# Products nobody reads, put into TensorE's long waits of a two-layer hybrid backbone

## The chip, the cores and the metric

The kernel is one program on one core of one Trainium2 chip. It is written against the engines directly: TensorE (PE in the profile, its weight loads PEld), VectorE (DVE), ScalarE (ACT), GpSimd (POOL) and SyncE (SP, which issues most DMAs) each have their own instruction list and meet only at semaphores. The metric is the device time of one execution in microseconds (us), from the first to the last instruction. Before the change it is 1954.93 us, the median of three runs (1952.61 to 1957.86).

## The reference

Two layers over 256 latent and 256 context tokens, width 1024. Each layer normalizes, projects to four mixers (attention, a long convolution by a Fourier transform, a 2-D Fourier mix, a gated delta rule), merges them and adds an MLP. Cut to what bears on the change:

```python
def rmsnorm(x, w):
    y = xf * lax.rsqrt(jnp.mean(xf * xf, axis=-1, keepdims=True) + EPS)
...
for li in range(DEPTH):
    mod = (jax.nn.silu(c) @ w_ada[li] + b_ada[li])[:, None, :]
    h = rmsnorm(x, norm1[li]) * (1.0 + sc1) + sh1
    p = h @ w_in[li]
    # hyena: the filter net sin(f1*(sin(f0*(feats@w1+b1))@w2+b2))@w3, its spectrum, then the convolution
    # gated delta: a_mat = strict(k k^T) * decay; t_mat = (a_mat + 1)^-1; states over chunks
    x = x + g1 * merge_branches(h, (ya, yb, yf, yd), ...)
    h2 = rmsnorm(x, norm2[li]) * (1.0 + sc2) + sh2
    x = x + g2 * sq_relu_mlp(h2, w_mlp1[li], w_mlp2[li])
```

The products that the change adds enter none of this: their results are read by nobody.

## The kernel before

Activations lie transposed: features on the 128 partitions, the 512 tokens (context first) along the columns. Large products are done three times over with operands split in a high and a low part (`mm3`, line 651); small ones as plain fp32 products (`mm`, line 646), which the profile shows as two records each. Transposes go through TensorE too (`turn`, line 757).

PSUM has eight banks. Four are unit banks, for the large products. Four are work banks, given out in turn by `fill(key)`: fill number n uses bank n % 4, and TensorE waits there until the reader of fill n - 4 has given that bank back (semaphores `work_free`; a reader calls `give_fill`). The reader of a fill waits on `filled`, a running count.

TensorE's order is written out by hand, and TensorE waits in order. The places that matter here:

- `start_`: transposes of the first vectors (`columns`), the first product of the filter net (`filter_angles(0)`, waits for its weights), modulation group 0, `filter_angles(1)` (waits for the sine of the first, made by DVE and ACT), group 1, eight transposes of x (fills read by ACT), the filter's taps (`filter_taps`, products with 64 rows), and then groups 2 to 7 with more filter work between them.
- `norm(li, which)`: three products with a matrix of ones sum the squares of x; ACT makes the inverse root; DVE, ACT and POOL make eight slices of h (`hhl`); TensorE's next large product waits for slice after slice (`h_ready`). The norms are numbered n = 2 * li + which, 0 to 3.
- `dn(li)`, the gated delta stage. `decay_row` and `key_products` fill banks that DVE empties (`far`, `key_matrix`), `decay_turned(e)` transposes eight matrices, which ACT copies out (`turned_copy`). DVE then solves 32x32 triangles in some sixty small steps (`solved_diagonal`), and `y_products` waits for it (`solved`). ACT must have done `turned_copy` 0 to 3 before it copies the second half of the diagonals, on which that solve waits.
- `between(chunk)` puts small work between the large products of `dn`; in layer 1 `decay_sums` waits there for the gates (`g_ready`).

Of the kernel before, what the change touches and what calls it, by code (L numbers as in the profile page):

```python
# [120 lines left out]
def build(nc, x, c, ctx, c_ctx, w_ada, b_ada, norm1, norm2, w_in, attn_qk_gain, attn_lambda, attn_subln,  # L121
# [3 lines left out]
    with es:  # L125
# [483 lines left out]
        def _(pe):  # L609
# [4 lines left out]
            def fill(key):  # L614
# [6 lines left out]
                return work_bank[n % WORK]  # L621

            def strip():

                n = n_strip[0]
                n_strip[0] += 1
                pe.wait_ge(S["lo_ready"], split_no[n] + 1)
                return whl[:, split_no[n] % RING]
# [16 lines left out]
            def mm(o_, a, b, start=True, stop=True):  # L645
                return nc.tensor.matmul(o_, a, b, start=start, stop=stop)  # L646
# [163 lines left out]
            def start_():  # L810
                pe.wait_ge(consts_loaded, 16)
                columns(0)
                filter_angles(0)
                pe.wait_ge(S["cT_ready"], 2)
                for g in range(FIRST_MODS):
# [20 lines left out]
            def norm(li, which):  # L836
                tk = toks(li) if which else slice(0, T)
                n = 2 * li + which
                b = fill(("ms", li, which))
                pe.wait_ge(S["sq_summed"], n + 1)  # L840
# [4 lines left out]
                pe.wait_ge(S["last_sq"], 2 * n + 1)  # L845
                mm(b[:, tk], ones, tmp[:, 0, tk], False, True).then_inc(filled, 1)

            def dn(li):
# [22 lines left out]

                def decay_sums():
                    pe.wait_ge(S["g_ready"], li + 1)
                    b = fill(("gcum", li))
# [52 lines left out]
                def between(chunk):  # L927
# [35 lines left out]
                    if chunk == 14:  # L963
                        key_products(0)
                    if chunk in (15, 16, 17):
                        decay_row(2 * chunk - 28)
                        decay_row(2 * chunk - 27)
                        key_products(chunk - 14)
                feature_strips("dn", li, h_part, between=between, part_ready=h_part_ready(li, 0))

                if li == 0:
# [9 lines left out]
                    key_products(3)  # L981
                    for e in range(8):
                        decay_turned(e)
                    token_strip("dz", li, 0)
# [119 lines left out]
                def read_out(st):  # L1104
                    for d in range(2):
                        m_ = MT[d][st]
                        if reads_out(li, m_):
# [3 lines left out]
                            heads(b, head_of(dnI[:, 4 * d + st, :]), head_of(dP3[:, d, :]))  # L1111

                y_products()
                if li == 0:
# [288 lines left out]
            def tail(li):  # L1403
# [4 lines left out]
                for hf in range(2):  # L1408
# [4 lines left out]
                    if li == 0 and hf == 0:  # L1413
                        vm_banks[:] = [work_bank[(n_fill[0] + a) % WORK] for a in (1, 2)]
                    with pe.Fori(0, 4) as i:
# [2187 lines left out]
```

## Time and profile before

| | |
|---|---|
| median of three runs | 1954.93 us |
| the profiled execution's own time | 1958.66 us |
| its span | 1956.8 us |
| PE busy | 1853.9 us, 95% of the span |
| DVE, ACT, POOL busy | 66%, 40%, 31% |
| chain that ended last | PE 71%, DVE 10%, issue 10%, POOL 4%, ACT 3% |
| mean granted TensorE clock | 0.980 |

PE busy says little by itself, since matmul records include the clock's slowness and the engine's pipeline. A row of the timeline gives start, duration, engine, line, operation, what is written and read, the shapes, the number of records, and in brackets how long the engine had been idle just before it and what released it. "PEclk" in a table of stretches is the granted clock as a share of full speed: 1.00 is 2.4 GHz and 0.50 is 1.2 GHz.

### The profile page before, as it was taken

To read this page: it belongs to the slowest core of one execution; us is meant where nothing else is said; L and a number is where in the kernel's file an instruction comes from. 1 tells how busy PE (TensorE), PEld (TensorE's weight loads), DVE (VectorE), ACT (ScalarE), POOL (GpSimd) and SP (SyncE) were. 2 spreads that over 40 slices of the span, in tenths; PEclk is the share of its full clock that TensorE was granted. 3 is DMA by queue.
4 is the path that set the end of the run, shared out by engine and by line. 5 is a ranking of instruction groups with operands and counts; after the bars stand their busy time and mean duration, and the time that the engine had idled before them with its cause. 6 is when DMAs were issued, how large, how long until landed. Compare 5 with 4: busy or idle time off the path is not lost.

```text
span 1956.8 us, 31847 instructions
## 1 busy us (share of the span) xinstructions
PE 1853.9 (95%) x11070; PEld 1520.0 (78%) x11070; DVE 1286.7 (66%) x2122; ACT 789.2 (40%) x1627; POOL 607.2 (31%) x553
## 2 busy tenths in 40 slices
PE   6999899999999999999999999898998899989999
PEld 2456788766588888777888887686787789989999
DVE  4855867666846765358765776859686655567574
ACT  2325534356243333333322322356435544445453
POOL 3333244622312121162300323434455421143020
PEclk8999999999999999999999999999999999999999
DMA  6433121332144453235556555222214335555554
GB/s 232 132 107 108 34 65 51 91 125 87 62 140 140 139 174 98 94 130 171 172 177 212 175 197 185 70 76 86 77 44 138 98 114 180 172 162 151 183 182 140
DMA packets 210925, 252.98 MB, mean 129 GB/s; under 512 B 11715, under 2 KB 176900, under 8 KB 209796
## 3 DMA queue, kind: packets, MB, share of 16 engines
q1 hardware_dynamic: 207088, 235.01, 38.0%
q10 hardware_dynamic: 3732, 16.60, 2.3%
q8 instruction: 61, 1.00, 0.2%
q14 instruction: 44, 0.36, 0.1%
HBM read 245.29 MB, written 6.29 MB: 129 GB/s over the span
## 4 chain that ended last, share of the span: by engine, by line
PE 71%; DVE 10%; issue 10%; POOL 4%; ACT 3%; DMA 1%; ACTq 1%; DVEq 0%; POOLq 0%
PE psum L651 57%; PE psum L646 12%; DVE big L2552 2%; POOL whl L1526 1%; DVE big L2561 1%; PE psum L757 1%; POOL big L3519 1%; DVE rstd L2552 1%; DVE big L2854 1%; ACT big L1765 1%; ACT whl L1517 1%; POOL big L3387 1%; ACT big L1768 1%; POOL big L1616 1%; DMA big<-in_hy_table_dram 1%
## 5 line engine op out<-in xcount | busy, mean ns | idle before, releaser
L651 PE MATMUL psum<-hhl,whl 128*128 128x512 f32 (+1 forms) x4416 | 835.1, 348 | 26.2 <-DVE hhl L2721 15.8
L651 PEld LDWEIGHTS psum<-hhl,whl 128*128 128x128 f32 x4416 | 701.0, 192 | 151.5 <-issue 42.5
L1517 ACT CAST whl<-raw 128x512 fp32r<-128x512 f32 x656 | 374.2, 618 | 838.6 <-PE psum L651 834.6
L1526 DVE TENSOR_TENSOR whl<-raw,whl 128x512 fp32r<-128x512 f32 x480 | 333.6, 736 | 320.8 <-ACT whl L1517 319.9
L651 PE MATMUL psum<-bigr,whl 128*128 128x512 f32 (+1 forms) x2688 | 475.2, 337 | 5.0 <-DVEq L3296 2.5
L651 PEld LDWEIGHTS psum<-bigr,whl 128*128 128x128 f32 x2688 | 412.6, 190 | 61.1 <-issue 6.9
L1526 POOL TENSOR_TENSOR whl<-raw,whl 128x512 fp32r<-128x512 f32 x176 | 233.2, 1347 | 382.1 <-ACT whl L1517 371.8
L646 PE MATMUL psum<-big 128*128 128x128 f32 (+8 forms) x1572 | 245.6, 330 | 21.7 <-DMA big<-in_hy_w_dram 5.5
L646 PEld LDWEIGHTS psum<-big 128*128 128x128 f32 (+4 forms) x1572 | 165.8, 179 | 78.8 <-issue 52.8
L3519 POOL TENSOR_TENSOR big<-big,tmp 128x512 f32<-128x512 f32 (+1 forms) x64 | 64.6, 1023 | 346.0 <-DVE tmp L3293 345.3
L651 PE MATMUL psum<-whl,hhl 128*128 128x512 f32 x672 | 160.0, 395 | 10.7 <-POOL whl L1526 8.7
L651 PEld LDWEIGHTS psum<-whl,hhl 128*128 128x128 f32 x672 | 125.5, 189 | 39.9 <-POOL whl L1526 11.9
L1768 ACT COPY big<-psum 128x512 f32<-128x512 f32 (+3 forms) x182 | 90.5, 498 | 104.4 <-PE psum L646 71.5
L1578 POOL TENSOR_TENSOR tmp<-tmp 128x512 f32<-128x512 f32 (+1 forms) x32 | 31.4, 980 | 321.3 <-ACT tmp L1765 321.3
L2704 DVE SCALAR_TENSOR_TENSOR big<-big,csil 128x512 f32<-128x512 f32 x112 | 87.3, 779 | 5.2
L1765 ACT ACTIVATE big<-psum 128x512 f32<-128x512 f32 (+3 forms) x142 | 66.0, 476 | 27.8 <-PE psum L646 12.1
L2685 DVE SCALAR_TENSOR_TENSOR big<-big,csil 128x512 f32<-128x512 f32 x84 | 64.3, 817 | 1.8 <-DVE tmp L3293 1.8
L3387 POOL TENSOR_SCALAR big<-xT,amp 128x256 f32<-128x256 f32 x48 | 53.9, 1134 | 36.4 <-issue 25.2
L2552 DVE TENSOR_TENSOR big<-psum,big 128x512 f32<-128x512 f32 (+2 forms) x74 | 47.5, 641 | 21.8 <-PE psum L646 18.9
L2556 DVE TENSOR_SCALAR big<-psum,cols 128x512 f32<-128x512 f32 (+1 forms) x48 | 31.8, 662 | 44.6 <-PE psum L651 27.7
L2561 DVE SCALAR_TENSOR_TENSOR big<-psum,cols,big 128x510 f32<-128x510 f32 (+1 forms) x96 | 58.4, 608 | 2.6
L757 PE MATMUL psum<-tab,big 128*128 128x128 f32 x296 | 46.3, 297 | 12.9 <-DVEq L1495 6.6
(185 smaller groups left out, 1473.0 us busy)
## 6 DMA issues: line engine op xcount, KB each, us to landing
raw<-in_w_mlp_dram SPq DMA_DIRECT2D x128, 512.0 KB, 3.8
raw<-in_w_in_dram SPq DMA_DIRECT2D x88, 512.0 KB, 3.6
big<-in_w_ada_dram SPq DMA_DIRECT2D x88, 512.0 KB, 5.0
raw<-in_w_gate_dram SPq DMA_DIRECT2D x64, 512.0 KB, 3.4
raw<-in_w_branch_dram SPq DMA_DIRECT2D x32, 512.0 KB, 3.4
raw<-in_w_ada_dram SPq DMA_DIRECT2D x24, 512.0 KB, 5.2
raw<-in_w_o_dram SPq DMA_DIRECT2D x16, 512.0 KB, 3.4
hy_spectra<-big ACTq DMA_DIRECT2D x2, 2560.0 KB, 9.4
```

What stands on the lines that cost most here:

```text
L646: return nc.tensor.matmul(o_, a, b, start=start, stop=stop)
L651: m = nc.tensor.matmul(o_, a(p_), b(q_), start=first and i == 0, stop=last and i == 2, skip_group_check=shared)
L757: m = nc.tensor.transpose(bank[:, i * P:(i + 1) * P], s, ids)
L1517: nc.scalar.copy(whl[:, r, 0, ks], raw_of(n)[:, ks]).then_inc(S["hi_ready"], 1)
L1526: ins = eng.tensor_tensor(whl[:, r, 1, ks], raw_of(n)[:, ks], whl[:, r, 0, ks].bitcast(F32), ALU.subtract)
L1765: return nc.scalar.activation(o_, i_, fn, **kw)
L1768: return nc.scalar.copy(o_, i_)
L2552: step(V.tensor_tensor(o_, a, b, op), s_)
L2561: step(V.scalar_tensor_tensor(o_, a, sc, b, op0, op1), s_)
L2704: ins = V.scalar_tensor_tensor(vm_acc if k == 7 else vm_part, w, c_, vm_part, MUL, ADD)
L3387: ins = G.tensor_scalar(hn[:, k, sl], xT[:, k, sl], amp[:, li, which, k, s_:s_ + 1], None, ALU.mult)
L3519: G.tensor_tensor(m_acc[:, i, tk], m_acc[:, i, tk], tmp[:, i % 2, tk], ALU.add)\
```

## The change

A helper `cover(key, n)` is added to TensorE's program. It takes a work bank as any fill does, runs n fp32 products of the 128x128 matrix of ones with 512 columns of the constant table into it, counts `filled` up by one at the last, and gives the bank back itself at once. It is called at thirteen places, 60 products in all: 11 and 4 around `filter_angles(0)`; after the sums of norms 0 to 3 (1, 8, 8 and 4), and 4 ahead of the sums of norm 3; in layer 0's gated delta stage 2 ahead of `decay_turned` 0, 2 and 4 each; in layer 1's 5 ahead of `decay_sums`, 6 after chunk 19, and 3 ahead of `y_products`. Nothing is removed, and no other engine's program changes except for the numbers of fills that it waits for. The two banks that the second modulation uses in the MLP are moved on by one, because the cover of norm 1 takes a fill number.

```diff
+            def cover(key, n, columns=512):
+
+                at = n_fill[0]
+                b = fill(("cover", key))
+                for _ in range(n):
+                    m = nc.tensor.matmul(b[:, 0:columns], ones, tab[:, 0:columns], start=True, stop=True)
+                m.then_inc(filled, 1)
+                pe.sem_inc(work_free[at % WORK], 1)
...
                 columns(0)
+                cover("start", 11)
                 filter_angles(0)
+                cover("angles", 4)
                 pe.wait_ge(S["cT_ready"], 2)
...
                 n = 2 * li + which
+                if n == 2 * DEPTH - 1:
+                    cover(("sums", n), 4)
                 b = fill(("ms", li, which))
...
                 mm(b[:, tk], ones, tmp[:, 0, tk], False, True).then_inc(filled, 1)
+                cover(("norm", n), (1, 8, 8, 4)[n])
...
                 def decay_sums():
+                    if li:
+                        cover(("gates", li), 5)
                     pe.wait_ge(S["g_ready"], li + 1)
...
+                    if chunk == 19:
+                        cover("strip", 6)
...
                     for e in range(8):
+                        if e in (0, 2, 4):
+                            cover(("turned", e), 2)
                         decay_turned(e)
...
+                if li:
+                    cover("solved", 3)
                 y_products()
...
-                        vm_banks[:] = [work_bank[(n_fill[0] + a) % WORK] for a in (1, 2)]
+                        vm_banks[:] = [work_bank[(n_fill[0] + a) % WORK] for a in (2, 3)]
```

The order of TensorE's instructions in the start-up, from the second product of `columns(0)` to the first taps, before (each row: line, operation, what is written and read, shape, number of products; the line numbers after the change are higher by 9 and more):

```order
L808 MATMUL psum<-tab,rows 128x52
L646 MATMUL psum<-big 128x256
L646 MATMUL psum<-raw,csil 32x256 x8
L646 MATMUL psum<-big 128x256
L646 MATMUL psum<-raw,csil 32x256 x8
L751 MATMUL psum<-tab,rows 128x128 x2
L757 MATMUL psum<-tab,big 128x128 x32
L646 MATMUL psum<-big 128x512 x4
```

And the same piece of TensorE's order after the change, where `raw,csil` are the modulation groups, `big 128x256` the two angle products and L766 the transposes of x:

```order
L817 MATMUL psum<-tab,rows 128x52
L628 MATMUL psum<-tab 128x512 x11
L655 MATMUL psum<-big 128x256
L628 MATMUL psum<-tab 128x512 x4
L655 MATMUL psum<-raw,csil 32x256 x8
L655 MATMUL psum<-big 128x256
L655 MATMUL psum<-raw,csil 32x256 x8
L760 MATMUL psum<-tab,rows 128x128 x2
L766 MATMUL psum<-tab,big 128x128 x32
L655 MATMUL psum<-big 128x512 x4
```

Eleven products (L628) now stand ahead of the first angle product, and four between it and modulation group 0.

The end of layer 0's decay rows and key products and the eight `decay_turned` on TensorE, before:

```order
L646 MATMUL psum<-tri_r,g_hl 128x128 x16
L646 MATMUL psum<-big 128x128 x8
L757 MATMUL psum<-tab,big 128x128 x32
L651 MATMUL psum<-whl,hhl 128x512 x48
L757 MATMUL psum<-tab,big 128x128 x8
```

The same place after the change, where 4 transposes make one `decay_turned`:

```order
L655 MATMUL psum<-tri_r,g_hl 128x128 x16
L655 MATMUL psum<-big 128x128 x8
L628 MATMUL psum<-tab 128x512 x2
L766 MATMUL psum<-tab,big 128x128 x8
L628 MATMUL psum<-tab 128x512 x2
L766 MATMUL psum<-tab,big 128x128 x8
L628 MATMUL psum<-tab 128x512 x2
L766 MATMUL psum<-tab,big 128x128 x16
L660 MATMUL psum<-whl,hhl 128x512 x48
```

Two products, and one fill of the ring of four, now stand ahead of the first, third and fifth `decay_turned`.

## Rows read from the trace of the kernel before

**Rows 1.** Table of five stretches: length, busy time of each engine (records), PEclk, DMA.
```profile
31.31:48.38 17.07, 17.07 (x59) 5.98 (x61) 12.67 (x18) 2.94 (x6) 11.15 (x9) 0.50 0.29 81
215.63:222.46 6.83, 4.96 (x22) 4.89 (x23) 4.73 (x11) 5.03 (x10) 0.00 (x0) 0.50 0.00 0
881.23:888.05 6.82, 5.75 (x14) 3.94 (x13) 6.82 (x10) 3.64 (x9) 3.68 (x3) 0.50 0.00 0
1389.81:1393.23 3.42, 3.42 (x128) 2.97 (x114) 2.86 (x5) 3.35 (x6) 0.63 (x1) 0.50 0.49 138
1758.45:1768.69 10.24, 7.40 (x28) 6.18 (x27) 7.96 (x15) 5.73 (x13) 5.41 (x6) 0.50 0.23 74
```
**Rows 2.** Timeline of PE alone, the start-up, 0 to 60 us.
```profile
7.30 0.35 PE L808 MATMUL psum<-tab,rows 52*128 52x52 f32 x1
13.17 1.22 PE L646 MATMUL psum<-big 33*128 33x256 f32 x2 [5.52 <-DMA big<-in_hy_w_dram]
...
18.43 1.22 PE L646 MATMUL psum<-big 128*128 128x256 f32 x2 [2.18 <-ACT big L1765]
...
25.97 2.76 PE L757 MATMUL psum<-tab,big 128*128 128x128 f32 x16 [0.88 <-ACTq L1495]
29.65 5.53 PE L646 MATMUL psum<-big 64*128 64x512 f32 x8 [0.92 <-DMA big<-in_hy_table_dram]
...
37.59 7.19 PE L646 MATMUL psum<-big 64*128 64x512 f32 x8
```
**Rows 3.** Timeline of PE alone, `filter_scale(0, 1)`: four products with the ones.
```profile
67.11 3.60 PE L646 MATMUL psum<-big,tab 128*128 128x512 f32 x8
```
**Rows 4.** Timeline of other engines in the start-up (ACTq: ACT issues a DMA).
```profile
19.68 0.45 ACTq L1798 DMA_DIRECT2D big<-in_hy_table_dram  x1
...
25.29 5.48 ACT L1768 COPY xT<-psum 128x512 f32<-128x512 f32 x8
...
68.29 8.79 POOL L3387 TENSOR_SCALAR big<-xT,amp 128x256 f32<-128x256 f32 x8 [25.21 <-issue]
```
**Rows 5.** Timeline of layer 0's `decay_turned` and of the solve that follows.
```profile
211.65 0.63 PE L757 MATMUL psum<-tab,big 128*128 128x128 f32 x4 [1.53 <-DVEq L1495]
...
215.00 0.63 PE L757 MATMUL psum<-tab,big 128*128 128x128 f32 x4 [1.88 <-DVEq L1495]
...
217.50 4.50 PE L757 MATMUL psum<-tab,big 128*128 128x128 f32 x20 [1.88 <-DVEq L1495]
...
255.47 2.11 DVE L2880 STREAM_TRANSPOSE big<-big 128x1024 f32<-128x1024 f32 x1
...
258.92 2.37 PE L646 MATMUL psum<-big 32*32 32x32 f32 x136
```
**Rows 6.** Timeline around norm 1, 872 to 893 us.
```profile
874.87 1.13 PE L646 MATMUL psum<-tmp,tab 128*128 128x512 f32 x2
...
880.48 2.27 PE L651 MATMUL psum<-hhl,whl 128*128 128x512 f32 x6 [4.49 <-DVE hhl L2721]
...
883.83 9.52 PE L651 MATMUL psum<-hhl,whl 128*128 128x512 f32 x32 [1.07 <-DVE hhl L2721]
885.38 1.66 DVE L2721 SCALAR_TENSOR_TENSOR hhl<-big,mod,hhl 128x256 fp32r<-128x256 f32 x4
```
**Rows 7.** Timeline of PE alone, layer 1's gated delta stage.
```profile
1293.45 0.85 PE L646 MATMUL psum<-small,tab 128*128 128x16 f32 x6 [3.13 <-DVE small L2815]
...
1329.85 13.69 PE L651 MATMUL psum<-hhl,whl 128*128 128x512 f32 x48 [3.92 <-POOL whl L1526]
...
1389.56 1.80 PE L646 MATMUL psum<-big 32*32 32x32 f32 x128 [2.42 <-DVE big L2880]
1391.29 6.65 PE L651 MATMUL psum<-whl,hhl 128*128 128x512 f32 x24
```
**Rows 8.** Timeline around norm 3, 1740 to 1776 us.
```profile
1763.61 12.61 PE L651 MATMUL psum<-hhl,whl 128*128 128x256 f32 x83 [2.84 <-DVE hhl L2721]
...
1765.47 1.35 DVE L2721 SCALAR_TENSOR_TENSOR hhl<-big,mod,hhl 128x256 fp32r<-128x256 f32 x2
```

## The prediction

> **What bounds the kernel now.** I read the table of stretches first, in fine steps, to find where the granted clock is 0.50: thirteen stretches, about 78 us together, of which [rows 1] shows five. In the first of them PE has work for all of its 17.07 us, in the others for most [rows 1]. That is what the change can win: where PE has work and is the limit, a stretch at 1.2 GHz costs half of its length; where another engine hands out the work, less. Then I read PE's timeline in and ahead of each of those places, for three things: how long PE waits there, what ends the wait, and whether the wait is long enough for the products put into it. Last the other engines at the same places, to see who is late once PE isn't.
>
> **Price of one product.** The same kind of product (ones by 512 columns, fp32) takes 3.60 us for four at the upper level, 0.88 each without the pipeline's tail [rows 3]. At the lower level the filter's taps, with as many columns, take 7.19 us for four, 1.8 each [rows 2]. Sixty products are 53 us at the upper level. They cost nothing only as far as they end before what PE waits for.
>
> **The start-up: +5.8 us.** PE is free at 7.65 and waits until 13.17 for weights, 5.52 us [rows 2]. Eleven products are 9.7 us at the upper level and 19.8 at the lower, so the first angle product starts at 17.3 to 27.5. At which level are they? The profile lists no change of the clock before 31.31, but the angle product at 18.43 takes 1.22 us for half of a tap's columns [rows 2], where half of a lower-level product is 0.9 and half of an upper-level one 0.44: the engine starts at 1.2 GHz. The Trainium skill ("TensorE: Matmul & The Clock Gate", Part 1, the HAM clock gate) says that the default state is the throttled one and that activity releases it. The row agrees with it, against the profile's clock column; by the column all eleven would be at 0.88 and the shift 2 us smaller than the one I take.
>
> I let the clock rise 4 us into the products (before the change it was up when x was transposed at 25.97, after no more work than that). Then they end near 19.4, and the angle product is 6.2 us late. The four products after it, 3.5 us, are hidden: from the first angle product to the second, 13.17 to 18.43, PE waits 2.18 us for the sine [rows 2], and the modulation group beside it gets quicker. So the second angle product, the sine after it and ACT's copies of x (25.29, [rows 4]) are about 6.2 us late too, and with the copies the later transposes of x, which ended at 28.73 [rows 2]: now 34.9. The spectrum table's DMA is issued behind the first modulation row, at 19.68 [rows 4]; 6 us later it has at most the 9.9 us that it took to the taps' start at 29.65, which makes 35.6 at the latest. The taps, which started at 29.65 after 0.92 us of wait [rows 2], start near 34.9: 5.3 late.
>
> Is the clock up then? Before, it fell at 31.31, after transposes paced by ACT, 0.88 and 0.92 us of waits and the first taps, and stayed at 0.50 though PE was busy without a gap, mostly with 64-row products, until 48.38 [rows 1, 2]. After the change PE comes to those transposes with a longer wait, not a shorter one: its own work ahead of them is quicker and ACT's copies are not. And no cover stands between there and the taps. So I expect the same fall and the same low stretch, and +0.5 for the piece of the taps that was still at the upper level (5.53 against 7.19 us, at most 1.6, [rows 2]). That is +5.8. Ends: the clock holds through the stretch, 5.3 - 17.07 / 2 = -3.2; a later rise in the covers, +8. Nothing behind absorbs it: modulation group 7, the scales and POOL's scaling at 68.29, which had been idle for 25.21 us [rows 4], all follow PE's order. One product after norm 0's sums: 0 to 0.9, taken as 0.1, because other ready work follows it and then a wait for h.
>
> **The turned matrices in layer 0: +2.6 us.** PE's waits of 1.53, 1.88 and 1.88 us [rows 5] look like room for three pairs, 1.76 us each. But their releaser is DVE giving back banks (line 1495), and a cover needs a bank as well. Now the first cover takes the bank that opened the first transpose at 211.65. The first two transposes take those that opened the second and third, the latter at 215.00; the second cover waits for the one that opened the fourth, at 217.50. So at 217.50, where PE had six matrices less one left to turn and all banks soon free [rows 5], it has still two pairs and six matrices: 3.5 us of products and six times 0.45 at the upper level. That is 223.7 instead of the 221.65 at which the large products began: +2.0. If the clock still falls there, the pairs are partly at 1.8 us each and it is +3.2. The engine was at 0.50 from 215.63, with transposes alone from 217.50, and rose at 222.46 [rows 1, 5]. The Trainium skill (same page, Part 4, PE-mode transpose) says that transposes don't count as busy for the clock. This row speaks against it; by that rule only the covers hold the clock here, the fall stays and I would take +3.2. I take 2.6. The other side doesn't hide it: ACT copies matrix 3 about 2 us later, so the solve ends later by as much. It ended at 257.58 while PE came at 258.92 [rows 5]: both move together.
>
> **Norms 1 and 2: -1.1 us each.** PE is free at 876.0 and waits 4.49 us; eight products end at 882.9, 2.4 us after the first slice of h at 880.48 [rows 6]. But PE waited again until 883.83, and the third slice comes at 886.2 (half into DVE's 1.66 us at 885.38). At 0.23 us a record ((4.22 / 2 + 5.30) / 32, [rows 1, 6]) the slices 0 and 1 end at 885.7, slice 2 at 887.6 and slice 3 at 889.0. Before, with the clock at 0.50 until 888.05, slice 1 ended at 886.6, slice 2 at 888.7, slice 3 at 890.1. So -1.1, and not the 2.1 that half of the 4.22 slow us would give. Norm 2 runs the same program over as many columns: -1.1 again. If the clock fell all the same, each would be +1.5.
>
> **Layer 1's gates, strip and solve: -0.1, 0, -0.8.** Five products are 4.4 us in a wait of 3.13 [rows 7]: 1.2 us over, against about as much saved on the slow products after it; ACT's splits follow, and DVE's solve is what the stage ends on. Six after chunk 19, 5.3 us in a wait of 3.92 at 1329.85 [rows 7]: PE wins up to 1.4 us and then waits 2.42 us for the solve at 1389.56 [rows 7] anyway, so 0; without that cover it would be -1.4. Three ahead of `y_products`, 2.6 us in 2.42: 0.2 over, against half of the 1.94 us that the 24 records at 1391.29 ran at 0.50, to 1393.23 [rows 1, 7]: -0.8.
>
> **Norm 3: -1.3 us.** The clock is at 0.50 for 10.24 us [rows 1]. Four products ahead of the sums and four after them let the sums end 0.2 us late and the first slice start at 1764.4 instead of 1763.61 [rows 8]. Slices of 0.73 us (0.12 a record, worked out as above) then meet the third slice at about 1766.2 [rows 8] and are through the fourth at 1767.7, which before was 1769.0.
>
> **Sum.** 5.8 + 0.1 + 2.6 - 1.1 - 1.1 - 0.1 - 0.8 - 1.3 = +4.1 us. Made against the profiled execution, 1958.66, it gives 1962.8; that one lies 3.7 us above the median of the three runs, and my number is for the median: 1954.9 + 4.1 = 1959.0. A measurement of this kernel can tell about 0.3% (5.9 us) from no change.
>
> **The rivals.**
> - *The start-up pays back* (0.22). The eleven products leave the clock up, and it holds through x and the taps: -3.2 in place of +5.8, so -4.9, 1950.0. For it: 8.5 us of loss in one stretch is the largest prize there is [rows 1]. Against it: ACT paces the transposes. With the turned stage at its low end and an earlier rise in the covers it reaches 1948. It decides from about 4 us saved in the stretch of 17.07. The Trainium skill's table of advice (same page, "Why this matters for your kernels") backs this rival: keep TensorE continuously busy to get the full clock.
> - *The delay at the start is absorbed* (0.12). If weights or tables, not PE, set the pace to 68.29, the start-up is 0 to +1: total -1.2, 1953.7. Against it: PE has work without a gap for the 17.07 us from 31.31 [rows 1], so it is PE that sets the pace there.
> - *The clock falls behind the covers all the same* (0.17). PE still waits after a cover for the next slice or copy, and if that short wait is enough for the clock to fall, the norms, the gates and the solve win nothing: 5.8 + 0.1 + 3.2 = +9.1, 1964.0; with the start-up at its upper end, +8, 1966.2. It ends on the slow side once two of the three norms' terms are gone.
> - *The forecast* (0.49): 1956.5 to 1962.5.
>
> **Chances.** Faster by over 0.3% (under 1949.1): the lower third of the first rival and some of what I can't see in the start, 0.13. Slower (over 1960.8): the third rival and somewhat over a third of the forecast, 0.35. Within: 0.52. The range 1949.5 to 1965.5 leaves out the tails of the first and third rival, some 0.2.
>
> **What would show it.** Start-up: first angle product near 19.4, taps near 35, a long stretch at 0.50 afterwards; if that stretch is gone, the first rival. Turned: the large products after it 2 to 3 us later relative to the last key product, waits still at DVE's releases. Norms: no stretch at 0.50 behind them, first slice 2.4 us later than its data. A stretch at 0.50 right behind a cover would make the terms of the norms wrong; a start-up late by under 3 us would make the whole wrong.

## The result: 17 us slower, outside the range

The changed kernel takes 1972.05 us (median of 5 runs, 1967.14 to 1975.78) against 1954.93 for the kernel before (median of 5 runs, 1950.68 to 1957.86). The ratio is 1.0091, 95% interval 1.0075 to 1.0107: 17.8 us slower (14.7 to 20.9), where I had said 4.1 and at most 10.6 (the medians differ by 17.1). The profiled execution took 1972.05 us, span 1970.1, mean granted clock 0.984 against 0.980 before. So the change did what it was made for, the clock is up for longer, and the kernel is slower all the same.

The covers are line 628. From the page's groups of instructions (busy time, mean ns, idle time ahead) of the changed kernel:

```profile
L628 PE MATMUL psum<-tab 128*128 128x512 f32 x120 | 57.4, 626 | 3.2 <-DVEq L1517 3.2
```

Stretches of the changed kernel, in the columns of [rows 1]. First six of its twelve at 0.50, then four behind norm 1, norm 2, layer 1's solve and norm 3, where PEclk was 0.50 before and is 1.00 now:

```profile
31.77:35.19 3.42, 3.03 (x14) 2.42 (x12) 0.00 (x0) 2.85 (x6) 3.19 (x4) 0.50 1.02 396
38.60:59.08 20.48, 20.48 (x70) 7.12 (x69) 12.13 (x21) 2.93 (x6) 8.33 (x7) 0.50 0.32 94
209.27:212.68 3.41, 3.41 (x18) 3.41 (x17) 2.89 (x7) 3.41 (x13) 1.12 (x1) 0.50 0.21 79
226.33:229.74 3.41, 3.02 (x4) 1.41 (x5) 2.02 (x6) 0.00 (x0) 0.00 (x0) 0.50 0.00 0
260.46:263.88 3.42, 3.42 (x10) 2.64 (x9) 3.20 (x7) 1.34 (x3) 1.10 (x1) 0.50 0.32 76
284.36:291.19 6.83, 6.54 (x94) 6.13 (x95) 2.75 (x4) 1.81 (x4) 0.00 (x0) 0.50 0.01 4
896.02:903.05 7.03, 7.03 (x18) 3.20 (x17) 5.68 (x9) 4.70 (x11) 6.18 (x5) 1.00 0.00 0
1268.52:1275.55 7.03, 7.03 (x18) 3.20 (x17) 5.79 (x10) 4.79 (x11) 2.68 (x3) 1.00 0.25 42
1404.96:1410.00 5.04, 5.04 (x140) 3.10 (x139) 4.78 (x5) 4.69 (x8) 2.51 (x2) 1.00 0.31 93
1770.24:1780.84 10.60, 9.83 (x37) 5.62 (x35) 6.62 (x12) 5.57 (x12) 7.83 (x9) 1.00 0.35 105
```

**The start-up.** PE's timeline, against [rows 2]:

```profile
7.51 11.57 PE L628 MATMUL psum<-tab 128*128 128x512 f32 x22
19.01 0.70 PE L655 MATMUL psum<-big 33*128 33x256 f32 x2
19.64 3.70 PE L628 MATMUL psum<-tab 128*128 128x512 f32 x8
23.27 1.07 PE L655 MATMUL psum<-raw,csil 128*32 128x256 f32 x16
24.27 0.70 PE L655 MATMUL psum<-big 128*128 128x256 f32 x2
...
31.28 3.52 PE L766 MATMUL psum<-tab,big 128*128 128x128 f32 x16 [3.20 <-ACTq L1517]
37.89 6.47 PE L655 MATMUL psum<-big 64*128 64x512 f32 x8 [3.09 <-issue]
```

The loads of the modulation weights as SP issued them in the kernel before:

```profile
15.46 6.49 SPq L1656 DMA_DIRECT2D raw<-in_w_ada_dram  x4
```

Then the changed kernel's DMAs in their own timeline and the view of the DMAs from 19 to 40 us (40 slices, then the median time from issue to landing), against [rows 4]:

```profile
23.97 2.66 SPq L1678 DMA_DIRECT2D raw<-in_w_ada_dram  x4
25.74 0.58 ACTq L1820 DMA_DIRECT2D big<-in_hy_table_dram  x1
```
```profile
GB/s 0 0 0 0 0 0 0 0 0 0 0 59 205 332 380 384 386 497 347 453 421 384 361 425 388 456 365 445 355 382 363 308 328 359 373 250 169 134 62 46
...
big<-in_hy_table_dram ACTq DMA_DIRECT2D x1, 512.0 KB, 12.1
```

The first angle product is 5.8 us late, as forecast (5.84), and so is ACT's issue of the spectrum table (19.68 before, 25.74 now). But the taps begin at 37.89 instead of 29.65, 8.2 us late, not 5.3. The idle time ahead of them is called "issue", that is, nothing the profile shows; 25.74 + 12.1 is 37.84, so it is the table. It takes 12.1 us and not 9.9. The loads of the modulation weights, which follow PE, now start together with it (SP issues four from 23.97; before, from 15.46), after some 5.8 us in which the DMA engines moved nothing (eleven slices of 0.525 us). That they are the reason is argued, not shown. For it: in s10 below the table is issued at 19.68 as before, only the loads are later, and it takes 12.1 us again. Against it: in s14 the table follows the loads as closely as here (20.66 and 22.44) and takes 10.8. Then the clock falls at 38.60 for 20.5 us with PE busy without a gap, where it was 17.07 [rows 1]. By 60 us the kernel is 9.2 us late, and 9.4 at 200 us.

**The turned matrices**, against [rows 5]. The second pair of covers runs at 1.2 GHz (0.50 from 226.33):

```profile
220.87 1.98 PE L628 MATMUL psum<-tab 128*128 128x512 f32 x4 [1.43 <-DVEq L1517]
...
226.72 3.47 PE L628 MATMUL psum<-tab 128*128 128x512 f32 x4 [1.78 <-DVEq L1517]
...
230.90 1.88 PE L628 MATMUL psum<-tab 128*128 128x512 f32 x4
232.62 1.91 PE L766 MATMUL psum<-tab,big 128*128 128x128 f32 x16
```

**Layer 0's small products.** I had no term for this place. PE stops for 2.18 us among 32x32 products, and nothing is late:

```profile
280.54 1.25 PE L655 MATMUL psum<-rstd,big 32*32 32x32 f32 x126
...
281.65 0.82 PE L655 MATMUL psum<-big,rstd 32*32 32x32 f32 x41
284.65 0.79 PE L655 MATMUL psum<-big,rstd 32*32 32x32 f32 x21 [2.18 <-issue]
```

**Norm 1**, against [rows 6]: no low stretch, the first slice 1.8 us later than its shift of 20.2, and then two waits for DVE's splits of the weights, which the trace before doesn't have there:

```profile
896.02 7.03 PE L628 MATMUL psum<-tab 128*128 128x512 f32 x16
902.49 3.33 PE L660 MATMUL psum<-hhl,whl 128*128 128x512 f32 x12
906.50 8.48 PE L660 MATMUL psum<-hhl,whl 128*128 128x512 f32 x36 [0.69 <-DVE hhl L2743]
915.34 5.73 PE L660 MATMUL psum<-hhl,whl 128*128 128x512 f32 x24 [0.37 <-DVE whl L1548]
...
921.80 3.48 PE L660 MATMUL psum<-hhl,whl 128*128 128x512 f32 x14 [0.37 <-DVE whl L1548]
```

These two waits don't come from the covers. s1 below has no product at this norm, its clock is at 0.50 from 891.62, and it has them too:

```profile
907.80 5.74 PE L660 MATMUL psum<-hhl,whl 128*128 128x512 f32 x24 [0.39 <-DVE whl L1537]
...
914.23 5.74 PE L660 MATMUL psum<-hhl,whl 128*128 128x512 f32 x24 [0.34 <-DVE whl L1537]
```

Laid side by side, the two traces part and close like this (how much later the same product starts, the covers left out of the count): start-up +9.4 by 200 us; turned matrices +2.9; a fall of the clock at 260.46 us +1.6; layer 0's small products, from 280 to 292 us, +4.8, of which the stop is 2.0 and most of the rest the stretch at 0.50 behind it; a fall of the clock at 376 us +1.6; in sum +20.2 at 400 us and up to norm 1. Then norm 1 +0.3, norm 2 -0.7; layer 1's gates, strip and solve -3.1; two falls of the clock that before's trace has near 1471 and 1519 us -2.8; norm 3 -1.0, less a fall at 1745 us that is new, +0.5; at the end +13.4. The traces place no more than these 13.4 us. Before's profiled execution is 3.7 us above its median, which is the arithmetic of the rest, not a place for it.

### The profile page after: what moved, and what is told of

Read it like the earlier page. It is cut to its first block, busy times and chain, and to the rows that moved or that the text cites. A ratio compares the mean times of both kernels' runs of the same rounds, so it can differ in the third digit from the quotient of the medians.

```text
span 1970.1 us, 32102 instructions
## 1 busy us (share of the span) xinstructions
PE 1896.5 (96%) x11190; PEld 1537.6 (78%) x11190; DVE 1281.1 (65%) x2122; ACT 789.3 (40%) x1627; POOL 607.6 (31%) x553
## 4 chain that ended last, share of the span: by engine, by line
PE 80%; DVE 8%; issue 4%; ACT 4%; POOL 3%; ACTq 0%; DMA 0%; DVEq 0%; SPq 0%; POOLq 0%
PE psum L660 64%; PE psum L655 12%; PE psum L628 2%; POOL whl L1548 2%; DVE big L2574 1%; PE psum L766 1%; ACT whl L1539 1%; ACT big L1787 1%; ACT big L1790 1%; DVE hhl L2743 1%; DVE big L2876 1%; DVE big L2583 1%; DVE whl L1548 1%; POOL big L1638 1%; DVE big L2726 1%
## 5 line engine op out<-in xcount | busy, mean ns | idle before, releaser
L660 PE MATMUL psum<-hhl,whl 128*128 128x512 f32 (+1 forms) x4416 | 824.5, 345 | 9.4 <-DVE whl L1548 3.7
L660 PEld LDWEIGHTS psum<-hhl,whl 128*128 128x128 f32 x4416 | 691.7, 190 | 130.2 <-issue 25.1
L628 PE MATMUL psum<-tab 128*128 128x512 f32 x120 | 57.4, 626 | 3.2 <-DVEq L1517 3.2
```

The lines of the kernel that those rows point to most:

```text
L628: m = nc.tensor.matmul(b[:, 0:columns], ones, tab[:, 0:columns], start=True, stop=True)
L660: m = nc.tensor.matmul(o_, a(p_), b(q_), start=first and i == 0, stop=last and i == 2, skip_group_check=shared)
```

## The experiments

Ratios are against runs of the kernel before on the same chip; one us is 0.0005. "Clock" is the mean granted clock over all runs of the version; the kernel before had 0.981 to 0.982 in them. The line numbers in the rows are each version's own. "A falls" says that theory A of the expectation is refuted. Each run has one trace, of one execution, which can lie some us off the median of its runs: totals are read from the runs, places from the traces.

**The change in parts.** Four versions of the changed kernel with some `cover(...)` calls taken out and nothing else:

```
s1:  keeps cover("start", 11), cover("angles", 4)
s2:  keeps cover("turned", e), 2 products each
s3:  keeps all but start and angles
s4:  keeps norms 1 to 3, sums, gates, strip, solved
```

> The kernel before with the eleven and the four products of the start-up alone. Theory A (the covers of the start-up carry the loss, because the spectrum table's DMA is issued 6 us later and then also takes longer): first taps at 37.9 us as in the changed kernel, 8.2 us later than before, and the total +9.3 us against the kernel before (1.0048). Theory B (my prediction's term, the loss beyond it lies elsewhere): +5.8 us (1.0030). Theory C (the delay is absorbed further on and all of the loss is in the other places): 0 to +1 us (1.0000 to 1.0005).

Measured (s1): 1.0067 (1.0045 to 1.0089), +13.1 us; clock 0.975. Above all three. The taps start at 37.77 and the trace is 9.2 us late at 60 us, as A had it, but its profiled execution is only 7.3 us behind before's: more than 5 us of the total stand in no trace.

> The kernel before with the three pairs of products among layer 0's turned matrices alone. Theory A (a cover takes a bank that DVE has not given back, so PE falls behind by two pairs and DVE and ACT with it): +2.0 us with the clock up, +3.2 with it down, and nothing behind takes it back: ratio 1.0010 to 1.0016. Theory B (the pairs are hidden, and the 3.2 us that the two traces differ by there come from where the clock falls): 0 to -1 us. Theory C (the later phase of layer 0 pays too, as the 11 us lost between 260 and 400 us in the changed kernel's trace would have it): +10 us or more.

Measured (s2): 1.0006 (0.9989 to 1.0024), +1.2 us. In the trace the stage is 3.1 us longer (200 to 223 us). C falls; A and B can't be told apart by the total. The traces speak for A: the stage is 1.4 to 3.1 us longer in the four that have these covers (the changed kernel, s2, s3, s12) and between 2.2 us shorter and 0.3 longer in the thirteen that don't.

> The changed kernel without the eleven and the four products of the start-up; all other covers stay. Theory A (the start-up costs 9.3 us): 9.3 us less than the changed kernel, about 1962 to 1963 us, that is +7 to +8 us against the kernel before (1.004). Theory B (my prediction's terms: the rest sums to 4.1 - 5.8 = -1.7 us): ratio 0.9991. Theory C (the rest loses 11 us in layer 0 and gives back 7 in layer 1, but the 11 came from clock falls that the start-up's shift had set off): -2 to -6 us, ratio 0.997 to 0.999.

Measured (s3): 1.0002 (0.9987 to 1.0017), +0.4 us; clock 0.991. The start-up is then 17 us of the whole change's 17.8, and A (+7 to 8) falls as well: all the rest together costs nothing measurable. B (0.9991) lies inside the interval.

> The changed kernel with the covers of norms 1 to 3, the gates, the strip and the solve alone: nothing at the start, after norm 0 and among the turned matrices. Theory A (these places win, as the 7 us that layer 1 gave back in the changed kernel's trace would have it): -4 to -7 us, ratio 0.9965 to 0.998. Theory B (the terms of my prediction): 0 - 1.1 - 1.1 - 0.1 - 0.8 - 1.3 = -4.4 us, 0.9977. Theory C (what they win in clock they lose in waits for DVE behind norm 1 and elsewhere, and the gain in that one trace was chance): 0 or slower, 1.000 or more.

Measured (s4): 0.998 (0.9965 to 0.9995), -3.9 us; clock 0.988. As both A and B had it; but see s9 and s16.

**What the start-up's loss consists of.** s5 and s6 issue the filter's tables early; s7 puts in three products where the change has eleven; s8 is s4 with early tables.

```
                     step(f(csil[:, :, s_], ..., ACT.Silu), S["cT_ready"])
+                load_filter_tables()
                 filter_sine(0)
...
                     if g == 0:
-                        load_filter_tables()
                         filter_sine(1)
```

> The kernel before with the eleven and the four products of the start-up, and with the three DMAs of the filter's tables issued by ScalarE ahead of the first sine instead of behind the first modulation row. Theory A (in the run with the start-up's covers alone the taps began at 37.8 us because the tables were issued 6 us later and took 12.1 us instead of 9.9): the tables are there first, ScalarE's copies of x set the pace, and the taps start at 34.9 us, 5.2 us later than before; the total is 3 us below that run, that is +6 us of delay and whatever the clock adds. Theory B (the tables are not the cause, the taps follow something else that moved): the taps start at 37.8 us again. Theory C (2.5 MB of tables ahead of x hold x up): taps later than 35.5 us.

Measured (s5): 1.0035 (1.0021 to 1.0048), +6.8 us, 6.3 less than s1 (their intervals just overlap: 4.1 to 9.4 against 8.8 to 17.4). PE in this run, from the transposes of x on:

```profile
31.88 3.37 PE L766 MATMUL psum<-tab,big 128*128 128x128 f32 x16 [3.26 <-ACTq L1506]
35.19 4.18 PE L655 MATMUL psum<-big 64*128 64x512 f32 x8
39.30 1.07 PE L655 MATMUL psum<-raw,csil 128*32 128x256 f32 x16
```

The wait ahead of the taps is gone, they start at 35.19 (A: 34.9), and the taps and the groups behind them run at the upper level (modulation group 1.07 us, not 1.93); the clock is at 0.50 only from 32.78 to 36.20 and from 46.44 to 53.27. By 60 us the run is 3.2 us late, not 9.2. So the late table cost its wait (the taps are 5.5 us late here, 8.1 in s1), and with it, in this trace, went the low clock of what comes behind; how far that is the table's doing one trace can't say (see the last section).

> The kernel before with the filter's tables issued early as in the run beside it, and no covers: the control for it. If the tables' DMAs cost nothing early, the taps start 0.9 us earlier than in the kernel before (their wait for the table goes) and the ratio is 0.9995 to 1.000. If they hold up x, whose transposes began at 21.9 us while the DMA engines were full until 29, the transposes begin 1 to 3 us later and the total is up to +3 us (1.0015).

Measured (s6): 0.9991 (0.9977 to 1.0005). x does come later (the transposes wait 3.62 us for its DMA and start at 25.69), yet the taps start at 31.51 without a wait, the clock stays up until 43.84, and at 60 us the trace is where before's is. Early tables alone don't win the 6.3 us of s5.

> The kernel before with three products at the start instead of eleven, and none behind the first angle product: at 1.8 us each they end by 13.0 us, before the weights that the first angle product waited for until 13.17. Theory A (the cost of the start-up's covers is the overrun, passed on one for one): first angle product within 0.3 us of before, the total within 1 us of before. Theory B (products there cost whatever their number, by what they do to the clock later): the start unchanged and the total still some us longer, with a mean granted clock below that of before. Theory C (a clock that is up earlier makes the start faster): the group at 14.32 us takes 1.07 instead of 1.93 us, and the total is up to 1 us shorter.

Measured (s7): 1.0004 (0.9989 to 1.0018), +0.8 us. The first angle product is 0.36 us later, the first groups run at 1.07 us as C said, and the clock then falls at 26.68, earlier than before, and stays down to 50.57. Being at the upper level early is lost again within 20 us. A holds, nearly; the clock, 0.979 against 0.981, is lower as B had it, but without a loss that could be measured.

> The version with the covers of norms 1 to 3, the gates, the strip and the solve alone, which took 0.998 of the kernel before, with the filter's tables issued early as well. If early tables win the 0.9 us that the taps waited, the ratio is 0.9975; if they hold up x, 0.998 to 0.9995. It is run as the candidate for the fastest version.

Measured (s8): 0.9985 (0.9972 to 0.9998); clock 0.991. No better than s4.

**Products that take little time.** The same calls with `columns=32` instead of 512.

> The covers of norms 1 to 3, the gates, the strip and the solve, as many products in the same places as in the run that took 0.998 of before, but each over 32 columns instead of 512, so that they take next to no time. Theory A (that run won by the clock): nothing is won, the granted clock is that of before and the low stretches behind the norms (from 881 and 1253 us in the trace of before) are back, ratio 0.9995 to 1.0005. Theory B (part of it came from where the program's instructions lie: before, PE stopped for 1.66 us with nothing to wait for among layer 1's 32x32 products at 1401.40, and in the kernel with sixty more cover records ahead of that place it did not): that stop is gone here too, and the ratio is 0.999, 1.5 to 2 us below before, with the clock as before.

Measured (s9): 0.9987 (0.9974 to 0.9999), -2.5 us, with the clock at 0.983 and the low stretches behind norms 1 and 2 still there (from 878.72 and from 1250.77, 3.4 us each). B. Layer 1's stop is 0.28 us.

> The fifteen products of the start-up in their places, each over 32 columns instead of 512. Theory A (the start-up's loss is the time of the products, passed on): first angle product at 13.2 and first taps at 29.7 us as before, total within 1 us of before. Theory B (the number of instructions, not their time, gives PE's stop of 1.6 to 2.0 us in layer 0's 32x32 products, which the three kernels with the start-up's covers had and no other): that stop is in this trace as well, with about 1,330 of the kernel's own product records ahead of it, and layer 1's stop is 0.3 instead of 1.66 us; layer 0's gated-delta stage then ends 1.5 to 2 us later than in before's trace and layer 1's wins as much back. If the stop goes with the time that PE waited and not with the count, there is none in layer 0.

Measured (s10): 1.0059 (1.0046 to 1.0072), +11.5 us; clock 0.977. A falls, and with it the picture of a loss made of product time:

```profile
7.68 4.90 PE L628 MATMUL psum<-tab 128*128 128x32 f32 x22
13.16 1.22 PE L655 MATMUL psum<-big 33*128 33x256 f32 x2 [0.59 <-DMA big<-in_hy_w_dram]
14.31 1.91 PE L628 MATMUL psum<-tab 128*128 128x32 f32 x8
...
31.83 6.93 PE L655 MATMUL psum<-big 64*128 64x512 f32 x8 [3.10 <-DMA big<-in_hy_table_dram]
```

The eleven end in time. The four behind the angle product take 1.91 us, so the first modulation group is done that much later, the loads that follow it too (SP at 17.30, before 15.46), and the table, issued at 19.68 as before, takes 12.1 us again: 2.2 us late, then 20.5 us at 0.50. And layer 0's stop is here, 1.61 us, and layer 1's is gone (0.27), as B had it. The total is open in part all the same: this profiled execution is the fastest of its five and ends only 2.6 us behind before's, so no trace shows where the rest of the 11.5 us lies.

> The covers of norms 1 to 3, the gates, the strip and the solve, early filter tables, three products at the start in the place of eleven, and four in the wait for x (3.62 us with early tables). If covers that end before what PE waits for are free and a clock that is up early helps, the start is 0 to 1.5 us shorter than without these seven, and the ratio is 0.997 to 0.998. If the start loses its clock later for it, as the run with three products alone did (0.50 from 26.68 to 50.57), the ratio is 0.9985 to 0.9995.

Measured (s11): 1.0001 (0.9988 to 1.0013); clock 0.989. That is outside both expectations: seven more products, all inside waits, won nothing, and more likely lost what the late covers had won (s8: 0.9985).

> The whole change, every cover in its place with as many products and its bank, but each product over 32 columns instead of 512. Theory A (the loss is the time of the products where they overrun): no loss at the start; among the turned matrices only the bank that each cover takes is left, at most half of the 3.2 us; the total 0 to +3 us, ratio 1.000 to 1.0015. Theory B (banks and instructions cost in themselves): turned stage +2 us or more, layer 0's stop among the 32x32 products 2.2 us as in the changed kernel, layer 1's 1.7 us, total +4 us, 1.002. Against before nothing of the clock's gain at the norms should be left in either.

Measured (s12): 1.0062 (1.0048 to 1.0075), +12.1 us; clock 0.977, stops of 2.09 and 1.86 us. So about a third of the change's 17.8 us is the length of its products (5.7 us, with some 3 us of uncertainty in each total). The turned stage is 2.1 us longer in the trace though its six products take next to no time: there the banks cost, as B had it. Neither theory had the start-up's part, for the reason that s10 shows.

**Where the stop stands, and single pieces.** s13 and s16 hold no product; s14 has the four behind the angle product, s15 the eleven over 32 columns.

```
s13, in place of cover("start", 11):
+                for _ in range(60):
+                    pe.wait_ge(consts_loaded, 16)
s16, at the end of norm(li, which):
+                if n in (1, 2):
+                    for _ in range(60):
+                        pe.wait_ge(consts_loaded, 16)
```

> The kernel before with sixty waits on a semaphore that is long there, put into PE's wait at 7.65 us, and no product at all. In the kernels with the start-up's covers PE stopped for 1.6 to 2.0 us, with nothing to wait for, 187 to 199 product records into layer 0's 32x32 products; in those with none ahead it was 217 records in and 0.2 to 0.3 us. Theory A (the stop stands at a fixed place of PE's instruction stream, and what is put ahead of it moves it into denser code): it moves back here as well, to some 180 to 205 records, and costs 0.5 us or more, with no product to explain it; layer 1's stop of 1.66 us shrinks or moves likewise. Theory B (it needs the products, their clock or their delay): it stays at 217 and 0.2 us. Total by A 0 to +3 us, by B 0.

Measured (s13): 1.0001 (0.9985 to 1.0017). Layer 0's stop has moved and grown, without a product, and layer 1's too (15 records earlier, 2.12 us instead of 1.66): A.

```profile
267.62 1.16 PE L655 MATMUL psum<-big,rstd 32*32 32x32 f32 x62
268.71 1.41 PE L655 MATMUL psum<-big 128*128 128x128 f32 x10
271.00 3.11 PE L655 MATMUL psum<-big 64*64 64x64 f32 x70 [0.87 <-issue]
```

In the kernel before, its 25 records of 128x128 end first and the stop is 0.18 us:

```profile
268.90 1.82 PE L646 MATMUL psum<-big 128*128 128x128 f32 x25
270.90 2.70 PE L646 MATMUL psum<-big 64*64 64x64 f32 x55 [0.18 <-issue]
```

> The kernel before with the four products behind the first angle product alone. My prediction had them hidden: PE waited 2.18 us for the sine behind the modulation group beside them, so nothing moves. Rival: they are not, because they stand ahead of that group, whose row releases ScalarE's DMAs of the filter's tables; at the lower level they take up to 7 us and at the upper 3.5, so the tables are issued 2 to 4 us later, the taps start that much later (at 32 to 34 us instead of 29.7), the clock falls in PE's wait for the table, and the total is +4 to +8 us.

Measured (s14): 1.0028 (1.0011 to 1.0044), +5.5 us; clock 0.978. The rival. The products stand from 14.35 for 5.68 us, the table is issued at 22.44 and the taps start at 33.31:

```profile
14.35 5.68 PE L628 MATMUL psum<-tab 128*128 128x512 f32 x8
19.96 1.07 PE L655 MATMUL psum<-raw,csil 128*32 128x256 f32 x16
...
33.31 5.06 PE L655 MATMUL psum<-big 64*128 64x512 f32 x8 [1.80 <-issue]
```

> The eleven products at the start, each over 32 columns, and none behind the angle product. In the run with all fifteen such products the eleven took 4.90 us, inside the wait of 5.5, so the start is not late here. If that run's +11 us came from the four behind the angle product (1.91 us, the tables 2.2 us later) and from the clock, this one is +1 to +3 us with layer 0's stop in it. If it came from the number of instructions, it is +8 us or more.

Measured (s15): 1.0012 (0.9997 to 1.0027), +2.3 us; no delay at the start (taps at 29.39), a stop of 1.28 us in layer 0. The first of the two.

> The kernel before with sixty satisfied waits behind the sums of norms 1 and 2 each, where PE waits 4.5 us for h, and no product. If the late covers' gain (0.998; with 32 columns 0.9987) is mostly that layer 1's stop of 1.66 us moves out of its 32x32 products, it is here too: ratio 0.999 and a stop of 0.3 us or none there. If it is the clock, the ratio is 1.000 and the stop unchanged or the low stretches behind the norms still there with nothing won.

Measured (s16): 0.9983 (0.9967 to 0.9999), -3.3 us, with the clock at 0.982, that of before. Layer 1 in the kernel before:

```profile
1398.98 0.76 PE L646 MATMUL psum<-big,rstd 32*32 32x32 f32 x37
1401.40 0.59 PE L646 MATMUL psum<-big,rstd 32*32 32x32 f32 x25 [1.66 <-issue]
```

and with the 120 waits:

```profile
1399.06 4.26 PE L655 MATMUL psum<-big 128*128 128x128 f32 x80
1403.60 2.08 PE L655 MATMUL psum<-big,tmp 64*64 64x64 f32 x64 [0.28 <-issue]
```

**The stop, over all versions.** Counted from the row of 126 products of 32x32 to the stop in layer 0:

| product records ahead of it that the version adds | records to the stop | stop, us |
|---|---|---|
| 0 (before, s4, s6, s8, s9, s16) | 217 | 0.02 to 0.47 |
| 6 (s7), 8 (s14), 12 (s2), 14 (s3), 14 (s11) | 210, 208, 204, 201, 202 | 0.51, 0.70, 0.69, 0.61, 0.27 |
| 22 (s15) | 195 | 1.28 |
| 30 (s1, s5, s10) | 187 | 1.61, 1.96, 1.61 |
| 44 (changed kernel, s12) | 171 | 2.18, 2.09 |
| none, but 60 waits (s13) | 202 | 0.87 |

Layer 1 has such a place too: 1.5 to 2.2 us in the kernel before, the changed kernel, s2, s6, s7, s12, s13 and s14, and 0.32 us or less in the other ten traces. There it stands at 167 records before, and at 160, 158, 153 and 152 in s7, s14, s2 and s13, so it moves by the same count. In s15, s1, s5, s10 and s16 the count would put it at 145 and 137, still among the 32x32 products, and there is no stop. (The stop of the changed kernel and s12, with 104 records ahead, stands at 184 and is a later place of the same kind.) So the products just ahead don't settle its cost alone, and what does stays open.

The view of the DMAs shows what comes ahead of it. From 281 to 285 us of the changed kernel only this moves:

```profile
q8 instruction: 1, 0.02, 1.4%
```

By the view's slices it begins at 282.2, and 1.4% of sixteen engines for 4 us is 0.9 us of one, so it ends near 283.1; PE goes on at 284.65. In the kernel before, such a DMA begins at 268.4 and at 1399.0, and PE goes on at 270.90 and 1401.40: about 2.4 us after the start of the DMA each time. That PE waits there for its instructions is my reading of these rows; the runs show that its place goes with the count, and needs no product. The Trainium skill ("Runtime: NRT & Kernel Launch", Instruction fetch mechanics) says that an engine's instructions are refilled in blocks of 256 by its own DMAs, and that crossing a boundary is mostly hidden. The rows agree that it mostly costs little, and show up to 2.2 us where the products are small.

## Why the prediction was wrong, step by step

- **Start-up, +5.8: the failed step.** Its first part held: covers at 1.2 GHz first and then faster, the angle product 5.84 us late. (The 4 us until the clock rose were luck: the row behind them doesn't show it, since PE had worked almost without a break from 18.43 to 25.97, over 6 us.) Wrong was "6 us later it has at most the 9.9 us that it took": the same 512 KB took 9.9 us before, 10.6 in s7, 10.8 in s14, 12.1 in the changed kernel, s1 and s10, and 14.6 in s5. With 12.1 us the taps came 8.2 us late instead of 5.3. Wrong, too, was "+0.5" for the clock: 3.4 and 20.5 us at 0.50 where there were 17.07. Together 9.2 us in the trace at 60 us, of which s5 gives 6 back by issuing the table earlier. The runs put more on the start-up's products than its first 60 us: 13.1 us alone (s1) and 17 with the others (s3).
- **"The four products after it, 3.5 us, are hidden."** No: s14, +5.5 us alone. I did not ask who waits for the group behind them. ACT's row copy and the weight loads do.
- **A term that was missing.** s1's trace is 3.5 us later again by 340 us: the stop of 1.61 us, and a fall of the clock at 270.40 behind a wait of 2.42 us for the solve. In the changed kernel the same place gives +6.4. I had only cost what the covers do on PE, not that they are instructions.
- **The parts don't add up, by the stop.** s1, s2 and s4 sum to +10.4 us, the whole is 17.8. s1 and s4 each end layer 1's stop (1.66 to 0.28 and 0.20 us, 1.4 us each); with both sets in, 104 records ahead, it is back at 1.71. That is 2.8 of the 7.4 us; the intervals of the four are 3 to 4 us wide each way, and the rest stays open.
- **Turned matrices, +2.6:** 2.9 in the changed kernel's trace, between my two values, with the fall of the clock that went with the upper one (226.33); 1.4 to 3.1 over the four traces with these covers. The reason held: s12 keeps the banks, takes the time out of the products, and is 2.1 us late there. The total of s2 (+1.2, -2.2 to +4.7) neither confirms nor refutes it. On the Trainium skill's rule that transposes don't count for the clock ("TensorE: Matmul & The Clock Gate", Part 4, PE-mode transpose): here too it was back at 1.00 at 229.74, but beside a cover, so this run can't decide it.
- **Norm 1, -1.1:** the clock came as forecast and PE was 0.8 us ahead by the fourth slice, but it gave that back to DVE's splits within 15 us, and the stage is +0.3. The step that failed is that PE sets the pace behind the slices. **Norm 2:** -0.7, but no gain of the covers can be read from it: in seven traces that have no product there (s1, s5, s6, s10, s13, s15, s16) the stretch at 0.50 merely begins earlier, and they gain the same 0.6 to 0.7 us on before's. What one trace loses at 0.50 depends on where the fall lies. **Norm 3:** -1.0 in all five traces with its covers over 512 columns, and 0 to +1.5 in the ten without any: here the forecast, -1.3, was nearly right.
- **Gates, strip, solve:** -0.3, -1.5 and -1.3 in the changed kernel's trace where I had -0.1, 0 and -0.8. The solve's -1.3 is no gain of its covers either: s1, s2, s5, s6, s7, s10 and s13 have none and show the same 1.3 us, because the fall of 1389.81 is missing in them. The total of s4, -3.9, is near my -4.4, but in part for another reason: layer 1's stop, 1.5 us of it, was no term of mine. s16, with the clock of before and no product, shows as much (-3.3 against -3.9 us), although s4 spends 27 us less at the lower level (from the mean clocks: 2 x (1 - 0.988) x 1955 = 47 us against 74). The stop explains some 1.4 us of s16 and the rest stays open; what the clock was worth lies inside the intervals.
- **The rivals.** "The start-up pays back" is refuted by s1; its best case, three products that end in time (s7), is +0.8. The Trainium skill's advice behind it, to keep TensorE continuously busy ("TensorE: Matmul & The Clock Gate", Why this matters for your kernels), held for the clock, 0.991 in s3, and gave no time: s3 is at 1.0002. "The clock falls behind the covers all the same" happened at the start and not at the norms.

## What to carry to other kernels

Work put into an engine's wait is free only if everything behind it is counted: who waits for the next instruction, which loads that one releases, and what those loads then share the DMA engines with. A higher granted clock is no gain in itself; ask which engine hands out the work at that place. Before crediting a small gain or loss to what was inserted, insert the same number of instructions that do nothing, and look at the same place in traces of versions that leave it alone.

## What the runs showed that I had not expected

- PE's stop at a fixed count of instructions, up to 2.2 us among 32x32 products, moved by sixty waits (thirty instructions) as well as by products. With 120 waits in norms 1 and 2, and nothing else, the kernel is at 0.9983 (0.9967 to 0.9999): the cheapest of the versions that came out faster than both kernels. s4 (0.998) isn't to be told from it, and with sixteen versions tried and an interval that ends at 0.9999 the gain itself wants a second measurement.
- An fp32 product over 32 columns isn't short: eleven (22 records) take 4.90 us with the clock low, against 11.57 for 512 columns, part of which ran with the clock up.
- The same start-up goes two ways. In seven traces with its instructions unchanged up to 60 us, but for waits, the clock fell near 31 to 32 us in five (for 6.8 to 20.5 us) and at 39.04 and 40.39 in two (6.8 us each), and those two were 2.7 to 3.1 us ahead of before's trace by 60 us. One profile of such a kernel places no difference under 3 us.
